# Two weight loads moved ahead of a transform's matrices, and the residual's input fetched by another engine's queue

## The reference, cut to what matters

```python
x = first_block(x, mem, ...)
    proj = rms_norm(x) @ w_in                       # four mixers from slices of it
    h = x + concat([ya, yb, yc, yd]) @ w_out        # <- the residual that reads x again
    h = h + memory_cross_attention(rms_norm(h), rms_norm(mem), w_xq, w_xkv, w_xo)
    h = h + conv_ffn(rms_norm(h), w_up, w_ffconv, w_down)
x = second_block(x, ...)
    g = hyena_filter(...)                           # filter taps, a small network and decays
    y = irfft(rfft(s) * rfft(g)) + s * skip         # rfft(g) is worked out early by this kernel
```

## Time and profile before

| | us |
|---|---|
| median of 3 runs | 1420.4 (1417.35 to 1421.86) |
| the profiled execution, its own time | 1420.73 |
| its span, first to last instruction | 1418.9 |
| TensorE busy | 1395.6 (98% of the span) |
| VectorE, ScalarE, GpSimd busy | 843.2, 556.4, 116.3 |
| mean DMA rate over the span | 101 GB/s |
| mean granted clock of TensorE | 0.994 of full speed |

### The profile page before, as it was taken

The page is one execution under the profiler, slowest core; times in us unless marked ns, Lnnn a source line. Parts: engine busy times, 40 slices in busy tenths (PEclk is TensorE's granted clock), DMA queues, the critical chain, the costliest instruction groups (busy, mean ns, idle before and its releaser), DMA issues.

```text
span 1418.9 us, 17485 instructions
## 1 busy us (share of the span) xinstructions
PE 1395.6 (98%) x6510; PEld 1124.7 (79%) x6510; DVE 843.2 (59%) x1151; ACT 556.4 (39%) x760; POOL 116.3 (8%) x137
## 2 busy tenths in 40 slices
PE   9999998999999999999999999999999999999998
PEld 7777785587888878888888888877888888888886
DVE  7757785264356864773576776767775434434445
ACT  6545684143334542431333544432234222213231
POOL 1010155000000000000000321014000000000000
PEclk9999999999999999999999999999999999999999
DMA  7232334422012323232222232341222232322221
GB/s 261 81 104 85 110 120 142 184 89 89 31 58 91 115 93 119 89 104 104 89 89 89 96 112 89 104 149 44 83 96 103 105 119 89 109 99 90 89 89 60
DMA packets 27590, 144.01 MB, mean 101 GB/s; under 512 B 3098, under 2 KB 8499, under 8 KB 12808
## 3 DMA queue, kind: packets, MB, share of 16 engines
q1 hardware_dynamic: 24040, 131.61, 26.4%
q0 software_dynamic: 2800, 10.82, 2.3%
q10 hardware_dynamic: 688, 0.73, 0.2%
HBM read 136.84 MB, written 6.30 MB: 101 GB/s over the span
## 4 chain that ended last, share of the span: by engine, by line
PE 90%; DVE 3%; DMA 2%; ACT 2%; issue 2%; SPq 0%; POOL 0%; POOLq 0%; DVEq 0%; ACTq 0%
PE ps L1836 27%; PE ps L1838 27%; PE ps L1837 27%; PE ps L2205 1%; PE ps L2261 1%; PE ps L2248 1%; DMA g_dram<-g_stage 1%; PE ps L2059 1%; DVE w_lo L1111 1%; ACT w_hi L624 1%; PE ps L2072 1%; DMA raw<-weights_dram 1%; PE ps L2050 0%; PE ps L2380 0%; PE ps L2382 0%
## 5 line engine op out<-in xcount | busy, mean ns | idle before, releaser
L1836 PE MATMUL ps<-opA_hi,w_hi 128*128 128x512 f32 x1120 | 443.0, 396 | 0.6 <-DVE w_lo L1111 0.4
L1838 PE MATMUL ps<-opA_hi,w_lo 128*128 128x512 f32 x1120 | 436.3, 390 | 0.0
L1837 PE MATMUL ps<-opA_lo,w_hi 128*128 128x512 f32 x1120 | 435.9, 389 | 0.0
L624 ACT CAST w_hi<-raw 128x2048 fp32r<-128x2048 f32 x111 | 211.6, 1908 | 293.6 <-PE ps L1838 284.5
L1111 DVE TENSOR_TENSOR w_lo<-raw,w_hi 128x2048 fp32r<-128x2048 f32 x112 | 256.9, 2293 | 115.5 <-ACT w_hi L624 113.7
L1836 PEld LDWEIGHTS ps<-opA_hi,w_hi 128*128 128x128 f32 x1120 | 210.4, 188 | 46.8 <-issue 2.8
L1838 PEld LDWEIGHTS ps<-opA_hi,w_lo 128*128 128x128 f32 x1120 | 210.2, 188 | 44.4
L1837 PEld LDWEIGHTS ps<-opA_lo,w_hi 128*128 128x128 f32 x1120 | 210.4, 188 | 43.9 <-issue 1.7
L1836 PE MATMUL ps<-opB_hi,w_hi 128*128 128x512 f32 (+1 forms) x584 | 228.5, 391 | 5.4 <-DVE opB_lo L1147 4.9
L1838 PE MATMUL ps<-opB_hi,w_lo 128*128 128x512 f32 (+1 forms) x584 | 226.3, 387 | 0.0
L1837 PE MATMUL ps<-opB_lo,w_hi 128*128 128x512 f32 (+1 forms) x584 | 225.9, 387 | 0.0
(11 more groups left out here) (377 smaller groups left out, 1414.1 us busy)
## 6 DMA issues: line engine op xcount, KB each, us to landing
raw<-weights_dram SPq DMA_DIRECT2D x113, 1024.0 KB, 4.8
g_dram<-g_stage POOLq DMA_DIRECT2D x8, 512.0 KB, 3.2
g_spec<-g_dram SPq DMA_DIRECT2D x5, 512.0 KB, 3.3
h<-x_t_dram POOLq DMA_DIRECT2D x1, 2048.0 KB, 9.7
h<-x_t_dram SPq DMA_DIRECT2D x3, 512.0 KB, 7.1
scores<-g_dram SPq DMA_DIRECT2D x3, 512.0 KB, 5.5
out_dram<-h SPq DMA_DIRECT2D x6, 256.0 KB, 2.3
mem_raw<-mem_t_dram POOLq DMA_DIRECT2D x1, 1024.0 KB, 8.8
```

What stands on the lines that cost most here:

```text
L624: A.copy(w_hi[:, p, :], raw[:, p, :]).then_inc(hi_ready, 1)
L1836: W.matmul(out, w[0], x[0], start=start, stop=False, skip_group_check=mixed)
L1837: W.matmul(out, w[0], x[1], start=False, stop=False, skip_group_check=mixed)
L1838: return W.matmul(out, w[1], x[0], start=False, stop=stop, skip_group_check=mixed)
```

## The change

SyncE's list gets the first two pairs of `w_out` (18 and 19) ahead of the wait for `masked` and of `g_fwd`. Behind `g_fwd` it gets the eight waits that stood on GpSimd, and the fetch of x into `h` in four transfers of 512 KB. The other pairs follow these. GpSimd's fetch and its waits go, and VectorE waits for four completions in place of one.

```diff
@@ SyncE
             load_pairs(FIRST["v_mem"] + 2, FIRST["w_out"])
+            load_pairs(FIRST["w_out"], FIRST["w_out"] + 2)
 
             sp.wait_ge(masked, 32)
             for q in range(2):
...
                     sp.dma_start(dst[:, :, r], src[:, :, r, 0:2, :]).then_inc(g_fwd_in, 16)
-            load_pairs(FIRST["w_out"], FIRST[f"up1_{FFN_ORDER[0]}"])
+
+            sp.wait_ge(gen_exp, 16)
+            sp.wait_ge(gen_done, 16)
+            sp.wait_ge(token0_done, 2)
+            sp.wait_ge(masked, 32)
+            sp.wait_ge(transposed, 32)
+            sp.wait_ge(biased, 16)
+            sp.wait_ge(token0_size, 2)
+            sp.wait_ge(g_patched, 2)
+            for i in range(4):
+                sp.dma_start(h[:, 2 * i:2 * i + 2, :], a["x_t"][:, 2 * i:2 * i + 2, :]).then_inc(x_again, 16)
+            load_pairs(FIRST["w_out"] + 2, FIRST[f"up1_{FFN_ORDER[0]}"])
@@ GpSimd
             fold(7, (2, 3))
 
-            pool.wait_ge(gen_exp, 16)
-            pool.wait_ge(gen_done, 16)
-            pool.wait_ge(token0_done, 2)
-            pool.wait_ge(masked, 32)
-            pool.wait_ge(transposed, 32)
-            pool.wait_ge(biased, 16)
-            pool.wait_ge(token0_size, 2)
-            pool.wait_ge(g_patched, 2)
-            pool.dma_start(h[:], a["x_t"]).then_inc(x_again, 16)
             for t in range(8):
@@ VectorE
-            dve.wait_ge(x_again, 16)
+            dve.wait_ge(x_again, 64)
             tail("w_out", "g_xa", 0, 1, 1)
```

## The result

The changed kernel took 1409.43 us (median of 4 runs, 1408.02 to 1410.41); the kernel before took 1420.61 beside it. The ratio is 0.9926, with a 95% interval of 0.9909 to 0.9943. In a later series on another occasion it was 1411.03 against 1419.62, ratio 0.9936 (0.9923 to 0.9950). The time moved by 11.2 us in the first and 8.6 in the other, so medians tell the size only to one or two microseconds; the traces tell it more closely.

What follows compares the result with a forecast made beforehand. TensorE, busy 98% of the span, was taken as the bound, so only its stops and half clock could give: 5.30 + 1.46 + 0.66 + 2.21 = 9.6 us off 1420.4, forecast 1410.8 us, 8 in 10 for 1408.2 to 1413.6.

Steps and rivals of the forecast that it cites:

- Pair 18: Ahead of unit 31's transposes: with the pair loaded early, ScalarE's 9.10 us wait and TensorE's whole 5.30 us stop go.
- What follows the stop at half clock: Between unit 31's transposes and the transform: no stop, so full clock; 0.51 + 0.95 = 1.46 us gained.
- The first product: The transform's first product takes 5.41 us at full clock in place of 6.07, a gain of 0.66 us.
- The second stop: Ahead of filter_spectrum(4): the first store into g_dram no longer stands behind x, so the 2.21 us stop goes.
- starts in place of ends: Reading the trace by TensorE's starts, since matmuls overlap, gives up to 0.6 us more gain.
- The time of x: On SyncE: x issued near 229.6 us; x and pair 20 done at 240 to 242, at 303 GB/s.
- pair 20: Sent at about 232 us behind x and split some 30 us after w_out's first products begin; costs nothing.
- rule on queues: At the first store: packet turns let it pass x, but its completion could come with x; 2.2 us at risk.
- Rival 2: Behind the first stop: the clock falls all the same as TensorE waits for the patches; gain 7.5, 1412.9 us; 6%.
- Rivals 1, 3 and 5: Late first store, 1412.8 us (12%); something else stopping unit 31, 1412.4 to 1414.4 (7%); no change, another wait (2%).
- Rival 4: At ScalarE's patches: matrices come late behind pair 19; slower only from a landing past 237.3 us; 2%.

Runs made afterwards that it cites:

- e2: The kernel before with only x moved to SyncE, in four pieces behind the matrices and pairs 18 and 19; 1417.95 us against 1419.15, ratio 0.9993.
- e1: The kernel before with only pairs 18 and 19 sent ahead of the matrices, x left on GpSimd; 1411.72 us against 1419.15, ratio 0.9948.
- e10: The changed kernel with only pair 18 ahead of the matrices, pair 19 behind them and ahead of x; one run at 1409.49 us.
- e3: The kernel before with 24 matmuls of ones, which nothing reads, in TensorE's first stop; 1422.25 us against 1419.15, ratio 1.0018.
- e5: e2 with 20 matmuls of ones in TensorE's first stop; 1417.52 us against 1419.62, ratio 0.9984.
- e9: e5 with 7 more matmuls of ones ahead of the values of units 30 and 31 and 4 behind; 1416.15 us against 1418.39, ratio 0.9981.
- e4: The changed kernel with one more wait on SyncE, so x goes at the moment of the first store into g_dram; one run at 1409.07 us.

## Why the prediction was right, and where its steps were not

The forecast was 1410.8 us, and 9.6 us of gain; measured were 1409.43, a gain of 11.2 us by the medians (8.6 in the later series), and 10.01 us in the stretch.

*Pair 18.* Right. With the pair ahead of the wait for `masked` and of the matrices the stop went whole. That the stop was as long as 5.30 us is in part the chance of one trace: pair 18's split was the latest of the five traces with a late pair 18, and e2 had a stop of 4.18. The forecast rests on that trace and so does the 10.01. e1 shows that this alone, with what follows from it, is 8.9 us, and e10 that one pair is enough.

*"What follows the stop at half clock", 1.46 us.* The size was right, and the reading of the kernel before incomplete. The start of the first product moved by 14.25 - 7.36 = 6.89 us, for 5.30 + 1.46 = 6.76 forecast. In the kernel before, what stood between the stop and that product was not only TensorE at half speed but also ScalarE's and VectorE's work queued behind the late split, 9.17 to 9.19 us of it whatever the clock (e2, e3, e5, e9). The step took the end of `token0_product(1)` at 234.42 for the releaser of ScalarE's chain at 234.46, and did not see that ScalarE's copy of unit 31's transposes ended there too, at 234.54. Two things ended within 0.12 us, and the one taken away by itself gave nothing. In the changed kernel ScalarE's queue is short and TensorE's end counts alone: ScalarE waits 0.47 us for `token0_product(1)` ahead of the row of token 0 and TensorE starts 2.36 us behind that product's end, where the forecast kept the 2.35 of the kernel before. At half clock that end would come about 1.46 us later (an estimate from the prediction's own rows; no run has the early pair and the half clock). So the sum came out because both went together, which the prediction had not argued: in that the step was lucky.

*The first product, 0.66 us.* Right: 6.07 to 5.41, and e9 shows 5.41 with the clock held.

*The second stop, 2.21 us.* Right in its cause, and a little short in size: from the second product to `w_out` it is 29.09 us before and 26.63 after, 2.46. That difference between idle time and starts is the "starts in place of ends" that was named. Here the two halves of the change are not independent: x alone takes away 2.46 us (e2), but once the pairs are ahead only 1.07 are left for x to take (e1), because GpSimd too waits for pair 18's split, and its x comes earlier with it.

*The time of x.* Right within a microsecond or two. The sum took 303 GB/s and had x and pair 20 in at 240 to 242. The four pieces of x, with a median of 5.5 us, were in at 236.6 and pair 20 at 239.1; 1.08 us of the difference is the earlier start of the whole stretch, and the transfers moved 420 GB/s from 231.3 to 236.8. The first store was issued at 235.9, 0.7 us ahead of x's end, and took 4.4 us where about 5 were assumed, most of it beside pair 20. The weighing of the rule on queues (the Trainium skill, DMA: Bandwidth & Descriptors, section Queues, rings and completion order) was hardly put to the test by the change itself. e4 did more: there the store, issued at 236.9, landed at 243.9, behind the first piece of x (241.4) and ahead of the last (247.7). So it did not wait for x as a whole, as taking turns would have it. What sets its 7.0 us, the sharing alone or the order of completions as well, this run does not tell.

*Rival 2, the clock.* It did not come, but what was said against it was weak. The 2.21 us stop had left the clock at 1.00, but in e5 it fell 1.0 us behind a wait of only 1.59 us, with TensorE at work again. The one wait of 1.33 us that is left in the changed kernel did not bring it down.

*Rivals 1, 3 and 5* did not come: the first store took 4.4 us, and nothing else stopped unit 31 or filled the two stops.

*Rival 4 and pair 20.* The matrices and pair 20 cost nothing, as forecast: SyncE had waited 1.1 us for the last mask when it issued the matrices, at 215.06.

## What to carry to other kernels

In a queue that is served in order, look at what the head waits for: a load whose slot had been free for 14 us stood behind a wait that had nothing to do with it, and moving it cost nothing here. When a stop is taken away, look at what ends within a tenth of a microsecond of the releaser, since that is what will be waited for next; and look at the next resource that is tied to other work than the waiting engine's, as the store behind x in e3, where 2.07 us less ahead of it (1.39 of them pair 18's earlier split) became 5.66 more. Filling an engine's waits with work that nothing needs held the clock in e9, with all three filled, and was worth 0.9 us there (a first product of 5.41 us against 6.29 in e2). With only the first filled the clock fell later (e3, e5), and the first product or product 4 paid for it with 8.23 and 8.42 us.

## What the runs showed of the hardware that was not expected

- TensorE's granted clock did not follow the length of the last wait alone. It stayed at 1.00 through waits of 2.21 (before), 1.33 (changed), 0.84 (e1), and 0.32 with 1.06 (e3). It went to 0.50 at the very end of the wait of 5.30 (before), 4.1 us into the one of 4.86 (e3), 0.4 us behind the end of the one of 4.18 (e2), and 1.0 us behind the end of one of only 1.59 (e5), the last two while TensorE was at work.
- The first product, or product 4, with the same matmuls (x12 in the rows), took 6.07, 6.29, 8.23 and 8.42 us where they began at half clock, by how late in them it came back, and 5.41 at full clock.
- A 512 KB store took 2.9 us alone, 4.4 beside the end of x and pair 20 on another queue, 7.0 beside all of x on another queue, and 9.7 to 12.2 just behind x in its own queue.
- The same instructions behind `w_out` took two values of span some 1.6 us apart from one profile to the next.
